# Sparse and latent attention of a three-block model: scale, bias and maximum of a head's scores in one VectorE instruction, one more unit of look-ahead, and the latent projections dealt out anew

## The reference, cut to what matters

```
s = einsum('bqhd,bkhd->bhqk', qb, k) * scale          # scale = d ** -0.5
s = where(allowed, s, -inf)                           # causal (latent), causal and top-128 selected (sparse)
p = softmax(s, axis=-1)
out = einsum('bhqk,bkhd->bqhd', p, v)
```

## Time and profile before

| | us |
|---|---|
| median of 3 executions | 3520.43 |
| the profiled execution's own time | 3521.64 |
| its span | 3519.80 |
| PE busy in the span | 3291.8 |
| DVE busy | 1692.3 |
| ACT busy | 1170.4 |
| POOL busy | 940.7 |
| mean granted PE clock | 0.963 |

### The profile page before, as it was taken

The page is one execution under the profiler, slowest core; times in us unless marked ns, Lnnn a source line. Parts: engine busy times, 40 slices in busy tenths (PEclk is TensorE's granted clock), DMA queues, the critical chain, the costliest instruction groups (busy, mean ns, idle before and its releaser), DMA issues. The chain is left out here.

```text
span 3519.8 us, 42159 instructions
## 1 busy us (share of the span) xinstructions
PE 3291.8 (94%) x17090; PEld 2630.1 (75%) x17090; DVE 1692.3 (48%) x2639; ACT 1170.4 (33%) x1877; POOL 940.7 (27%) x405
## 2 busy tenths in 40 slices
PE   6999989988999899999999776989999889999998
PEld 4877767866888688888878665358888766678887
DVE  6995576554332323345520698454221378752211
ACT  3233464324443422122232223333222233643222
POOL 0001313432444232322322000013444221024443
PEclk8999999998999999999999999889999899999999
DMA  5222424451223222343421000012233212013332
GB/s 203 96 95 86 159 78 163 152 176 60 96 95 95 81 84 91 120 138 127 149 72 60 31 19 13 1 42 85 99 98 106 65 54 63 1 60 96 97 95 90
DMA packets 91789, 315.99 MB, mean 90 GB/s; under 512 B 10822, under 2 KB 12614, under 8 KB 90314
## 3 DMA queue, kind: packets, MB, share of 16 engines
q1 hardware_dynamic: 88876, 304.74, 26.4%
q10 hardware_dynamic: 2720, 8.55, 0.7%
HBM read 311.16 MB, written 2.10 MB: 89 GB/s over the span
## 5 line engine op out<-in xcount | busy, mean ns | idle before, releaser
L266 POOL TENSOR_TENSOR terms<-streams,terms 128x1024 fp32r<-128x1024 f32 (+2 forms) x401 | 940.5, 2345 | 2559.7 <-ACT terms L254 2559.7
L525 PE MATMUL banks<-terms,terms 128*128 128x512 f32 (+2 forms) x3776 | 1408.5, 373 | 24.9 <-POOL terms L266 10.1
L526 PE MATMUL banks<-terms,terms 128*128 128x512 f32 (+2 forms) x3776 | 1403.2, 372 | 0.0
L527 PE MATMUL banks<-terms,terms 128*128 128x512 f32 (+2 forms) x3776 | 1401.7, 371 | 0.0
L254 ACT ACTIVATE terms<-streams 128x1024 fp32r<-128x1024 f32 (+1 forms) x462 | 475.4, 1029 | 1713.3 <-PE banks L527 1496.0
L525 PEld LDWEIGHTS banks<-terms,terms 128*128 128x128 f32 x3776 | 716.5, 190 | 159.2 <-issue 30.4
L527 PEld LDWEIGHTS banks<-terms,terms 128*128 128x128 f32 x3776 | 716.5, 190 | 121.8
L526 PEld LDWEIGHTS banks<-terms,terms 128*128 128x128 f32 x3776 | 717.0, 190 | 119.7
L2011 DVE TENSOR_TENSOR stage<-stage,banks 128x256 f32<-128x256 f32 (+1 forms) x84 | 51.9, 618 | 543.4 <-ACT stage L1989 543.4
L1346 DVE SCALAR_TENSOR_TENSOR arena<-arena,vec 128x512 f32<-128x512 f32 x240 | 162.5, 746 | 0.2
L1975 DVE TENSOR_TENSOR terms<-stage,terms 128x512 fp32r<-128x512 f32 (+1 forms) x66 | 114.3, 1735 | 0.0
(11 more groups left out here) (391 smaller groups left out, 3395.8 us busy)
## 6 DMA issues: line engine op xcount, KB each, us to landing
streams<-in_ffn_w SPq DMA_DIRECT2D x104, 512.0 KB, 3.5
streams<-in_w_mod SPq DMA_DIRECT2D x72, 512.0 KB, 3.5
streams<-in_w_up SPq DMA_DIRECT2D x44, 512.0 KB, 3.5
streams<-in_w_gu SPq DMA_DIRECT2D x44, 512.0 KB, 3.5
streams<-in_w_ada SPq DMA_DIRECT2D x32, 512.0 KB, 3.5
streams<-in_w_down SPq DMA_DIRECT2D x32, 512.0 KB, 3.5
streams<-in_w_v SPq DMA_DIRECT2D x24, 512.0 KB, 3.7
streams<-in_ffn_w SPq DMA_DIRECT2D x24, 384.0 KB, 3.3
```

The costliest lines, as they stand in the source:

```text
L266: gp.tensor_tensor(self.low(m), self.raw(n), self.high(m), ALU.subtract).then_inc(self.low_made.sem, 1)
L525: pe.matmul(out, high[:, at], x_high, start=kk == start, stop=False)
L526: pe.matmul(out, high[:, at], x_low, start=False, stop=False)
L527: mm = pe.matmul(out, low[:, at], x_high, start=False, stop=kk == kts - 1)
```

## The change

Four things are changed, all in the third block:

1. `biases`: L3513/L3517 and L3522 give way to one `tensor_tensor_reduce` per head, which writes -scale * (score + bias) to `s` and the running minimum of it to `top`. It shows on DVE as a main instruction and a read of the accumulator. The exponential takes scale = -1, so its result is as before. The signal that PE waits for before it overwrites scores is now `biased`, the same that ACT waits for.
2. Look-ahead: step i now does transposed(i-3) and sums(i-4) on PE, move(i-3) and keep(i-4) on ACT; `s` and `first` have four buffers.
3. `Latent`: the 19 outputs come in the order r r k k q v v k k q v k k q v k k q v, the turns come after outputs 3, 4 and 5, and ACT evicts v as well. ACT begins the pass with an exponential of one column, so that the table for exp is loaded there and not at the first L3484.
4. `values_three` runs 4 selection rounds beside each of its 4 pieces, not 5: 16 there, and 5 (not 1) at the end of `Latent.vector`.

```diff
-A3_PT0 = A3_ROWS + 6 * T3
+A3_PT0 = A3_ROWS + 8 * T3
...
     def read(self, n):
-        return self.k.dve_done(max(2 * n, 1))
+        return self.biased(n + 1)
...
     def tensor(self, pe):
...
-        for i in range(self.N + 3):
+        for i in range(self.N + 4):
             if i < self.N:
                 self.score(pe, i)
-            if 2 <= i < self.N + 2:
-                self.transposed(pe, i - 2)
-            if i >= 3:
-                self.sums(pe, i - 3)
+            if 3 <= i < self.N + 3:
+                self.transposed(pe, i - 3)
+            if i >= 4:
+                self.sums(pe, i - 4)
...
-            s = self.s[:, n % 3, e, :w]
-            ins = act.activation(s, s, ACT.Exp, bias=self.top[:, n % 4, e:e + 1], accum_out=self.total[:, n % 4, e:e + 1])
+            s = self.s[:, n % 4, e, :w]
+            ins = act.activation(s, s, ACT.Exp, scale=-1.0, bias=self.top[:, n % 4, e:e + 1], accum_out=self.total[:, n % 4, e:e + 1])
...
     def biases(self, dve, n):
...
-        if n >= 3:
-            dve.wait_ge(*self.turned(n - 2))
+        if n >= 4:
+            dve.wait_ge(*self.turned(n - 3))
...
-        if self.wide(n):
-            for e in range(2):
-                ins = dve.scalar_tensor_tensor(s[:, e, :].rearrange("p (c t) -> p c t", c=2),
-                                               self.scores(n)[:, 2 * e:2 * e + 2, :], scale,
-                                               bias.rearrange("p (c t) -> p c t", c=2), ALU.mult, ALU.add)
-        else:
-            ins = dve.scalar_tensor_tensor(s[:, :, :w], self.scores(n), scale,
-                                           bias.rearrange("p (o t) -> p o t", o=1).to_broadcast([P, 2, w]),
-                                           ALU.mult, ALU.add)
-        ins.then_inc(k.dve_done.sem, 1)
-        dve.wait_ge(*self.read(n))
-        dve.tensor_reduce(self.top[:, n % 4, :], s[:, :, :w], AX.X, ALU.max, negate=True).then_inc(self.biased.sem, 1)
+        for e in range(2):
+            shape = "p (c t) -> p c t" if self.wide(n) else "p (o t) -> p o t"
+            x = self.scores(n)[:, 2 * e:2 * e + 2, :] if self.wide(n) else self.scores(n)[:, e:e + 1, :]
+            ins = dve.tensor_tensor_reduce(s[:, e, :w].rearrange(shape, t=x.shape[-1]), x,
+                                           bias.rearrange(shape, t=x.shape[-1]), -scale, 3.0e38, ALU.add, ALU.min,
+                                           self.top[:, n % 4, e:e + 1])
+        ins.then_inc(self.biased.sem, 1)
...
-    outs = [("r", i, 0) for i in range(2)] + [("v", t, 0) for t in range(len(KEYS))]
-    outs += [("q", g, 0) for g in range(4)] + [("k", g, c) for g in range(4) for c in range(2)]
+    outs = [("r", 0, 0), ("r", 1, 0), ("k", 0, 0), ("k", 0, 1), ("q", 0, 0), ("v", 0, 0), ("v", 1, 0), ("k", 1, 0),
+            ("k", 1, 1), ("q", 1, 0), ("v", 2, 0), ("k", 2, 0), ("k", 2, 1), ("q", 2, 0), ("v", 3, 0), ("k", 3, 0),
+            ("k", 3, 1), ("q", 3, 0), ("v", 4, 0)]
     banks = [3, 4, 5, 0, 1, 2]
-    turns_after = {1: 0, 2: 1, 3: 2}
+    turns_after = {3: 0, 4: 1, 5: 2}
...
     def scalar(self, act):
         half = T3 // 2
+        act.activation(self.k.unused[:, :], self.k.eps[:, 0:1], ACT.Exp)
         for n, (kind, i, c) in enumerate(self.outs):
-            if kind == "v":
-                continue
...
+            else:
+                rows = KEYS[i][1] - KEYS[i][0]
+                if i == 0:
+                    act.activation(self.v[32:32 + META, i, :], b[:META, :], ACT.Copy)
+                ins = act.activation(self.v[:rows, i, :], b[:rows, :], ACT.Copy)
...
     def vector(self, dve):
         selection = self.mixing.selection
-        for n, values in enumerate(((0, 1), (2,), (3, 4))):
+        for n in range(3):
             self.rope(dve, n)
-            for t in values:
-                self.value(dve, t)
...
-    values = values_three(k, lambda kk, t: src(kk, KEYS[t]), lambda dve, m: selection.rounds(dve, 5))
+    values = values_three(k, lambda kk, t: src(kk, KEYS[t]), lambda dve, m: selection.rounds(dve, 4))
```

More of the change, by code:

```diff
@@ L3370, in __init__ @@
         self.counts = {s: self.N for s in signals}
-        self.counts.update({k.dve_done: 2 * self.N, k.act_done: 8, k.parted: 8})
+        self.counts.update({k.dve_done: self.N, k.act_done: 8, k.parted: 8})
     def query(self, n, e):
@@ L3492, in scalar @@
     def scalar(self, act):
[L3493 to L3497, removed]
+        for i in range(self.N + 4):
+            if 3 <= i < self.N + 3:
+                self.move(act, i - 3)
+            if i >= 4:
+                self.keep(act, i - 4)
             if i < self.N:
                 self.exponentials(act, i)
-            if i >= 3 and (i - 2) % self.group == 0:
-                self.highs(act, (i - 2) // self.group - 1)
+            if i >= 4 and (i - 3) % self.group == 0:
+                self.highs(act, (i - 3) // self.group - 1)
     def biases(self, dve, n):
@@ L3528, in norms @@
         dve.reciprocal(both, both).then_inc(k.dve_done.sem, 1)
-        dve.wait_ge(*k.dve_done(2 * n + 3 if n + 1 < self.N else 2 * self.N))
-        dve.tensor_tensor(self.first[:, n % 2, :].rearrange("p (e c) -> p e c", e=2)[:, :, :META],
-                          self.s[:, n % 3, :, :META],
+        dve.wait_ge(*k.dve_done(n + 1))
+        dve.tensor_tensor(self.first[:, n % 4, :].rearrange("p (e c) -> p e c", e=2)[:, :, :META],
+                          self.s[:, n % 4, :, :META],
                           both.rearrange("p (e o) -> p e o", o=1).to_broadcast([P, 2, META]), ALU.mult)
         for e in range(2):
-            s = self.s[:, n % 3, e, META:w]
+            s = self.s[:, n % 4, e, META:w]
             ins = dve.tensor_scalar(s, s, both[:, e:e + 1], None, ALU.mult)
@@ L3549, in vector @@
                 self.norms(dve, i - 1)
[L3550 to L3551 removed]
+            if i >= 5 and (i - 4) % self.group == 0:
+                self.lows(dve, (i - 4) // self.group - 1)
         self.lows(dve, 3)
 class Latent(Pass):
[L3558 to L3559 removed]
+    outs = [("r", 0, 0), ("r", 1, 0), ("k", 0, 0), ("k", 0, 1), ("q", 0, 0), ("v", 0, 0), ("v", 1, 0), ("k", 1, 0),
+            ("k", 1, 1), ("q", 1, 0), ("v", 2, 0), ("k", 2, 0), ("k", 2, 1), ("q", 2, 0), ("v", 3, 0), ("k", 3, 0),
+            ("k", 3, 1), ("q", 3, 0), ("v", 4, 0)]
     banks = [3, 4, 5, 0, 1, 2]
[L3561 to L3562 removed]
+    turns_after = {3: 0, 4: 1, 5: 2}
     def __init__(self, k, mixing, values):
@@ L3571, in __init__ @@
         self.w_k, self.w_v = k.arena[:, B3_UKV:B3_UKV + 512], k.arena[:, B3_UKV + 512:B3_UKV + 1024]
-        self.made, self.kept, self.turned, self.swapped, self.cosined, self.roped, self.taken = k.more[9:16]
+        self.made, self.kept, self.turned, self.swapped, self.cosined, self.roped = k.more[9:15]
         self.placed = k.averaged
-        n, v = len(self.outs), len(KEYS)
-        self.counts = {self.made: n, self.kept: n - v, self.turned: 3, self.swapped: 3, self.cosined: 3, self.roped: 3,
-                       self.taken: v, self.placed: 1}
+        n = len(self.outs)
+        self.counts = {self.made: n, self.kept: n, self.turned: 3, self.swapped: 3, self.cosined: 3, self.roped: 3,
+                       self.placed: 1}
     def bank(self, n):
@@ L3583, in bank_there @@
         if n >= 6:
-            self.read(pe, n - 6)
+            pe.wait_ge(*self.kept(n - 5))
         elif self.banks[n] < 3:
             self.values.evicted(pe, 0, self.banks[n])
[L3588 to L3593, removed]
     def out(self, pe, n):
@@ L3673, in rope @@
         dve.tensor_tensor(x, x, t, ALU.add).then_inc(self.roped.sem, 1)
-    def value(self, dve, t):
-        n, rows = self.from_v + t, KEYS[t][1] - KEYS[t][0]
-        dve.wait_ge(*self.made(n + 1))
-        if t == 0:
-            dve.tensor_copy(self.v[32:32 + META, 0, :], self.bank(n)[:META, :])
-        dve.tensor_copy(self.v[:rows, t, :], self.bank(n)[:rows, :]).then_inc(self.taken.sem, 1)
     def vector(self, dve):
         selection = self.mixing.selection
-        for n, values in enumerate(((0, 1), (2,), (3, 4))):
+        for n in range(3):
             self.rope(dve, n)
-            for t in values:
-                self.value(dve, t)
         dve.wait_ge(*self.roped(3))
```

11 lines of the change are left out of this document (5 added, 6 removed).

## The result

The changed kernel took 3497.27 us, the median of 4 executions (3495.14 to 3501.99), against 3520.64 for the kernel before (3520.22 to 3521.39): a ratio of 0.9932, interval 0.9916 to 0.9947, so 23 us or 0.7% faster. A later measurement gave 0.9940 (0.9923 to 0.9957). The forecast was 3506.0, with a range of 3498.5 to 3514.5: right in direction, too small by nine of twenty-three microseconds. The profiled execution took 3497.28 us, its span 3495.5.

The account below looks back on a forecast made before the run. No engine was full; PE, DVE and ACT waited for each other. Terms -3.6, -7.8, +1.0 and -4.0 made -14.4 us on the profiled 3521.64, 3507.2; the median, 1.2 lower, 3506.0, range 3498.5 to 3514.5.

Parts of the forecast that it names:

- Bounds of the kernel before: Third block's attention: no engine full, they wait for each other; PE needs 22.3 of 25.91 us a group, 3.6 are waits.
- Entry: Latent stage up to the first biases: these start at 2984.15, not 2987.76, bounded by DVE; -3.6 us.
- New instruction: Fused bias and maximum on DVE: 1.41 us a wide unit, 8.1 us a group; DVE's load falls from 21.6 to 16.2.
- Three groups at full clock: Attention's steady groups: each loses 3.6 us of waits and gains 1.0 of new ones; -7.8 us in all.
- new waits: Steps behind the wide units, where ACT's work lies between PE phases: 1.0 us lost in a group.
- look-ahead: Attention loop: with three steps, transposed(i-3) finds its norms done a step earlier and PE's phases cover DVE.
- First group: Attention's first group: runs at half clock, is PE's alone, gains nothing and pays the filling; +1.0 us.
- A low stretch of another length: Half-clock stretch at the start of attention: a length other than 19 us was listed as showing the prediction wrong.
- Tail: The 12.51 us after the last score: one more unit in hand covers the last norms, no half clock; -4.0 us.
- Sum: Third block's latent stage and attention: all terms together -14.4 us.
- The rival of the early clock: Attention: low clock lasts 5.6 us, not 19.4, winning half of 13.8; -21.3 us, 3499.1; chance 15%.

Follow-up runs that it names:

- old_latent: The change with the old latent stage and 5 selection rounds beside each piece of w_vs put back: 3503.36 us, ratio to before 0.9961.
- latent_alone: The kernel before with only the new latent stage, ACT's v evictions and 4 rounds beside w_vs: 3514.33 us, ratio to before 0.9993.
- no_lag: The change with the old look-ahead of two steps and three row buffers: 3496.13 us, ratio to before 0.9941.
- ttr_alone: The kernel before with only the new DVE instruction: 3499.84 us, ratio to before 0.9955.
- rounds19_no_lag: The change with two-step look-ahead and 5, 5, 5 and 4 rounds beside the w_vs pieces, 2 left: 3496.03 us, ratio to before 0.9935.
- warm_after: The change with six unread 512-column matmuls on PE between score 1 and score 2: 3487.34 us, ratio to before 0.9927.
- warm_before: The kernel before with five unread 512-column matmuls on PE after the last k output: 3517.67 us, ratio to before 0.9998.

## Why the prediction was off

- **Bounds of the kernel before**: the waits were where the prediction put them, on norms, but 2.8 us a group and not 3.6. PE's own need of a group was put at 22.3 us; it is 22.9, with PE busy for 22.7.
- **Entry, forecast -3.6**: -3.4 (30.7 to 27.4), old_latent and latent_alone agree. What bounds it now was foreseen: DVE's rounds end last, ACT has time to spare. But against the second and third profile of before it is -2.3 (29.7), for the low stretch of the latent stage, which the sum left out, is in the 30.7. The table load in the new place cost next to nothing: the weights of turn 1 waited 0.2 us for ACT's eviction of r, and PE's matmuls went on without a pause.
- **New instruction**: 1.27 us a wide unit against 1.41, DVE 15.6 a group against 16.2. The nearest row was the right one. The Trainium skill's rule of half throughput ("Vector Engine (DVE) Microarchitecture Reference", Points that are easy to get wrong) is not tested by it, one source being PSUM here; the row with two fp32 SBUF sources, 1.15 us for 1024 elements, shows no halving.
- **Three groups at full clock, forecast -7.8**: -9.8 (78.6 to 68.8), of which 0.9 is the low clock that reached into the first of them. The 1.0 us of new waits a group did not come; 0.2 is left, and PE's own need was put 0.6 too low. The reason given was wrong in part: the step "look-ahead" claimed the waits for itself, while no_lag and ttr_alone show that the shorter DVE step alone removes them all, and the look-ahead alone 1.0 of 3.0, since it trades the waits for norms for waits of the wide scores.
- **First group, forecast +1.0**: -7.1. This is the step that failed. It took the half-clock stretch of 19.4 us as given. A low stretch of another length was among the prediction's own signs of being wrong. From the first bias instruction to score 6, before ran 17.0 us at half clock, the change 5.7. At half a us lost for each, the price that the prediction used, that is -5.7. The runs give less: the two profiles of rounds19_no_lag differ by 17.1 us of low clock and 7.4 us of stage, 0.43 each; in the first group the change and warm_after by 5.7 and 1.3, before and warm_before by 13.6 and 4.8. From these I estimate before's loss at 4.8 to 6.5 us and the change's at 1.3, so that the clock has 3.5 to 5.2 of the 7.1. The look-ahead moved 1.75 us out of this group; the rest is the shorter DVE step's.
- **Tail, forecast -4.0**: -1.0. Without the look-ahead it is -3.0 (14.6), the low clock and the waits gone as foreseen; the unit more that the look-ahead leaves behind costs 2.0, which the step overlooked. It counted the extra work as cover for the last norms and not as work after the last score.
- **Sum**: stage -21.2 against -14.4. The rival of the early clock, given 15%, had -21.3: the clock did come back early, in 6.8 us, but that the sums agree is luck. Against the rival's terms the groups gave 2.0 us more, the first group 1.2 more, and the tail 3.0 less. Its chance was too low, because I read 97% busy PE in the low stretch as a sign that nothing in the order could end it.
- **Ahead of the stage**: -3.1, in code that is the same. The first eviction lies at 2944.6 to 2959.0 us over eighteen profiles, and the forecast had no term for it. Five profiles reach it before 2948 us; they have 198 to 208 us of low clock ahead of 2945, the other thirteen 215 to 246. Yet before has 225 there and the change 232, so the 3.1 between these two stay unexplained. Without them the time would have been 3500.4, inside the range: that it fell outside is in part chance. The median of before was 3516.8 to 3520.6 in the five series, and the later ratio of 0.9940 would have put the time at 3499.3, also just inside.

Why the clock comes back after 7 us in one order and 17 in the other stays open. Versions with the new instruction or the look-ahead, the entry at 27 us or later and no fillers had 6.8 to 13.7 us in eight profiles of six kernels; the old attention 17 to 24 in four profiles of two; early entries without fillers 0, 17 and 24. The attention's order seems to matter, by the first two sets, and chance does, by the third; no run separates the two further.

## What to carry to other kernels

When engines wait for each other in a loop, shorten the step that the loop goes through before deepening the pipeline: here one fused instruction made the fourth buffer useless, and the deeper pipeline sent its gain at the start on to the tail. A stretch at half clock in the row before is a term of the sum with several values (none to 24 us here), not a constant; price them, and expect that an edit which moves PE's pauses may pick another. Measure from a point of the trace that both kernels share, for code ahead of it may shift by itself, here by up to 14 us. And judge by many executions when the clock has a hand in it: one profile may show a gain of 7 us that ten runs do not.

## What I had not expected of the hardware

- With unread matmuls in a pause of 5.3 us, one profile had PE at full clock through the attention's first units (1.00 over 13.4 us), where three profiles of the same kernel without them had 6.8 to 10.2 us at half clock. It is one profile, and rounds19_no_lag had none in one of two without any filler, so that the fillers do it is likely and not shown.
- The same instruction stream ran 17.1 us at half clock in one execution and at full clock in another, with 65 and 127 matmul instructions done.
- A load of ScalarE's table was followed by an activation after 0.02 us (2958.27 to 2958.29).
- Deeper look-ahead removed 2.8 us of waits for norms from a group and brought 1.9 us of others.
- The fused instruction over PSUM and SBUF needs 0.64 us for 528 fp32 elements with the minimum, and two in a row overlap by 0.07 us.
